# Two value matrices and the head gates share one product after the first phase, and the keys move into it

## The reference, cut to what matters

```python
u = rms_norm(h, norm1_g[layer]) * (1 + scale1) + shift1
z = u @ w_in[layer]
q_a, kc, vc, ksl, vsl, kwn, vwn, g_a, q_b, k_b, v_b, m_a, m_b = jnp.split(z, split_at, axis=-1)
k_slc = rms_norm(ksl.reshape(kv_shape), k_norm_g[layer, 1])
k_win = rms_norm(kwn.reshape(kv_shape), k_norm_g[layer, 2])
g_nsa = jax.nn.sigmoid(g_a).reshape(B, S, NSA_KV_HEADS, NSA_GROUP, 3)
y_a = nsa_attention(q_a, k_cmp, v_cmp, k_slc, vsl..., k_win, vwn..., g_nsa, rel_bias) @ w_up_nsa[layer]
y_b = stick_breaking_attention(q_b, k_b, v_b) @ w_up_sb[layer]
```

## Time and profile before

| | |
|---|---|
| runs | 1045.01 us median of 3 (1043.51 to 1045.26) |
| profiled execution | 1043.5 us, its span 1041.8 us |
| busy in the span | PE 1023.6, PEld 931.7, DVE 803.8, ACT 615.9, POOL 49.2 us |
| granted TensorE clock | 0.997 of full speed |
| traffic | 209.46 MB, mean 201 GB/s |

### The profile page before, as it was taken

One profiled execution on the slowest core, in us unless ns is written; L12 is line 12 of the kernel. 1 busy time (PEld: TensorE's weight loads), 2 busy tenths in 40 slices (PEclk: granted clock), 3 DMA queues, 4 the chain that ended last, 5 costly groups with the idle time before them and its releaser, 6 DMA issues.

```text
span 1041.8 us, 18924 instructions
## 1 busy us (share of the span) xinstructions
PE 1023.6 (98%) x6894; PEld 931.7 (89%) x6894; DVE 803.8 (77%) x1478; ACT 615.9 (59%) x1145; POOL 49.2 (5%) x74
## 2 busy tenths in 40 slices
PE   6999999999999999999999999999999999999998
PEld 5999998999988888888888889899999998888887
DVE  6997988888998655598887768667877968888753
ACT  5488788446555454565664457795654466655532
POOL 1011100020100000000000100000000020000000
PEclk9999999999999999999999999999999999999999
DMA  9997755677866666666566545545334556566663
GB/s 365 415 354 266 259 187 182 212 242 245 294 193 190 185 193 188 182 185 193 189 186 194 186 143 162 162 151 172 124 122 143 164 161 201 182 189 195 183 190 114
DMA packets 58507, 209.46 MB, mean 201 GB/s; under 512 B 7055, under 2 KB 8463, under 8 KB 57912
## 3 DMA queue, kind: packets, MB, share of 16 engines
q1 hardware_dynamic: 52616, 185.24, 55.5%
q0 software_dynamic: 5808, 23.09, 6.3%
HBM read 205.14 MB, written 3.16 MB: 200 GB/s over the span
## 4 chain that ended last, share of the span: by engine, by line
PE 89%; DVE 5%; ACT 3%; DMA 1%; issue 1%; SPq 0%; DVEq 0%; ACTq 0%
PE bank L691 88%; DVE ring_rounded L1859 2%; PE bank L1038 1%; ACT rounded_rounded L1406 1%; DVE ada_ring L1915 1%; DMA ring<-in_stream 1%; DMA ada_ring<-in_ada 1%; ACT body L1565 0%; DVE x L2224 0%; DVE body L2013 0%; DVE x L2223 0%; DVE x L2151 0%; DVE body L2063 0%; DVE body L2137 0%; DVE body L2087 0%
## 5 line engine op out<-in xcount | busy, mean ns | idle before, releaser
L691 PE MATMUL bank<-u_rounded,rounded_rounded 128*128 128x256 f32 (+1 forms) x2152 | 506.8, 329 | 1.7 <-DVE ring_rounded L1859 1.3
L1859 DVE TENSOR_TENSOR ring_rounded<-ring,rounded_rounded 128x1024 fp32r<-128x1024 f32 x326 | 395.8, 1222 | 117.0 <-ACT rounded_rounded L1406 104.8
L1406 ACT ACTIVATE rounded_rounded<-ring 128x1024 fp32r<-128x1024 f32 x326 | 342.0, 1054 | 107.9 <-PE bank L691 83.3
L691 PE MATMUL bank<-u_rounded,ring_rounded 128*128 128x256 f32 x1504 | 351.0, 281 | 0.0
L691 PEld LDWEIGHTS bank<-u_rounded,rounded_rounded 128*128 128x128 f32 x2152 | 333.0, 188 | 5.1 <-issue 1.5
L691 PE MATMUL bank<-body_rounded,rounded_rounded 128*128 128x256 f32 (+1 forms) x1296 | 322.4, 336 | 2.4 <-ACT body_rounded L1718 2.3
L691 PEld LDWEIGHTS bank<-u_rounded,ring_rounded 128*128 128x128 f32 x1504 | 283.0, 188 | 37.0
L691 PE MATMUL bank<-body_rounded,ring_rounded 128*128 128x256 f32 x952 | 217.3, 280 | 0.0
L691 PEld LDWEIGHTS bank<-body_rounded,rounded_rounded 128*128 128x128 f32 x1296 | 201.8, 189 | 4.3 <-ACT body_rounded L1718 2.5
L691 PEld LDWEIGHTS bank<-body_rounded,ring_rounded 128*128 128x128 f32 x952 | 179.0, 188 | 26.3
L1662 ACT ACTIVATE part<-bank 128x256 f32<-128x256 f32 x65 | 24.9, 383 | 78.9 <-PE bank L691 78.9
(11 more groups left out here) (269 smaller groups left out, 885.9 us busy)
## 6 DMA issues: line engine op xcount, KB each, us to landing
ring<-in_stream SPq DMA_DIRECT2D x328, 512.0 KB, 3.7
ada_ring<-in_ada POOLq DMA_DIRECT2D x32, 512.0 KB, 5.2
body<-in_ada SPq DMA_DIRECT2D x8, 512.0 KB, 9.0
ada_ring<-in_ada SPq DMA_DIRECT2D x6, 512.0 KB, 8.4
mem_parts_kept<-body_rounded POOLq DMA_DIRECT2D x2, 1024.0 KB, 6.7
body_rounded<-mem_parts_kept POOLq DMA_DIRECT2D x2, 1024.0 KB, 5.1
x<-in_x_t SPq DMA_DIRECT2D x2, 512.0 KB, 4.7
body<-in_mem_t SPq DMA_DIRECT2D x2, 512.0 KB, 7.0
```

The source lines that it names most:

```text
L691: return nc.tensor.matmul(out, lhs, rhs, start=start, stop=stop, skip_group_check=True)
L1406: a(R(slot_round(q)), slot_weights(n), ACT.Copy).then_inc(slot_rounded, 1)
L1859: v.tensor_tensor(R(w), w, R(slot_round(q)), ALU.subtract).then_inc(slot_split, 1)
```

## The change

The keys `ks` and `kw` take the place of the sparse values in the first phase, in the same slots and with as many matmuls of 256 columns. After it `project_packed` makes the sparse values and the gates in one go, 128 + 128 + 24 = 280 moving columns, three blocks `k` to a slot, so that slots 16 to 18 now hold these. The gates come out with tokens on the partitions, so `ga_turn` falls away. `mem_ss` is made halfway in that product. Banks 0, 1, 2 go by the shorter `proj_names`: bank 0 now holds `x_ss`, `vsb0`, `vsw0`, `qa1`, `cmp_hid_k`, and `qa0` takes the place of `qa1` in bank 7, behind `mem_ss`. GpSimd loads the bias diagonals behind the memory's stores.

```diff
-FIRST_BANKS = {"vsb0": 0, "vsb1": 1, "vsw0": 2, "vsw1": 2, "kc": 3, "vc": 3, ...
+FIRST_BANKS = {"vsb0": 0, "vsb1": 1, "ks": 2, "kw": 2, "kc": 3, "vc": 3, ...
+AFTER_FIRST = {"vsw0": 0, "vsw1": 1}
-    out = ["ga", "ks", "kw", "qa0", "qa2", "qa3"]
+    out = ["qa1", "qa2", "qa3"]
     out += ["cmp_hid_k", "cmp_hid_v", "ma0", "cmp_turn_k", "cmp_turn_v"]
-    out += ["ga_turn", "ma1", "cmp_out_k", "cmp_out_v", "ma2", "ma3", "ma4"]
+    out += ["ma1", "cmp_out_k", "cmp_out_v", "ma2", "ma3", "ma4"]
+            def project_packed(names, k, lhs, halfway):
+                ps = [claim(n) for n in names]
+                hi, lo = lhs
+                for i in range(k):
+                    if i == k // 2:
+                        halfway()
+                    if i % PACK == 0:
+                        chunk = at["chunk"]
+                        w_hi, w_lo = take(SLOT)
+                    c = slice(i % PACK * PACKED, (i % PACK + 1) * PACKED)
+                    for t in range(TT):
+                        at_t = slice(t * P, (t + 1) * P)
+                        ins = mm(ps[t][:, 0:PACKED], R(hi[:, i, at_t]), w_hi[:, c], i == 0)
...
+                        mm(ps[t][:, 0:PACKED], R(hi[:, i, at_t]), w_lo[:, c])
+                        ins = mm(ps[t][:, 0:PACKED], R(lo[:, i, at_t]), w_hi[:, c], stop=i == k - 1)
-            project("ga", KD, u_parts)
-            project("ks", KD, u_parts)
...
-            project("kw", KD, u_parts)
+            project_packed(("vsw0", "vsw1"), KD, u_parts, sum_memory)
             sum_squares("ks", "halves")
...
             load_ada(0, ADA_RING)
-            pool.wait_ge(bias_stored, 16)
-            pool.dma_start(bias, ...).then_inc(loaded["bias"], 16)
             load_ada(ADA_RING, ADA_RING + ADA_IN_KEYS)
...
             pool.dma_start(mem_parts_kept[1], R(mem_n_lo)).then_inc(mem_stored, 16)
+            pool.wait_ge(bias_stored, 16)
+            pool.dma_start(bias, ...).then_inc(loaded["bias"], 16)
...
             for t in range(TT):
-                output(f"vsw{t}")
...
                 spread_heads(pair_v[:, t, :, :], f"vsb{t}")
+            ahead("kc", 5)
             for w, n in enumerate(("kc", "vc")):
...
-            copy(gate_raw, "ga", bank("ga")[0:24, 0:T])
+            ahead("kc", 6)
+            square("ks")
+            square("kw", T)
             key_blocks(0)
-            square("ks")
-            row_inv("mem_ss")
-            square("kw")
+            row_inv("mem_ss", 1)
+            ahead("kc", 7)
+            for t in range(TT):
+                output(f"vsw{t}", 3)
...
             key_blocks(2)
             inv_rms("ks", HD, None)
```

More of the change, by code:

```diff
@@ L43 @@
 SLOT = 8
+GA = 24
+PACKED = 2 * P + GA
+PACK = SLOT * P // PACKED
 RAW_GATES = 4
@@ L115, in stream_chunks @@
     for k in range(KD):
-        for c in (C_VS, C_VW, *(C_VB + j * P for j in range(4)), C_KC, C_VC):
+        for c in (C_KS, C_KW, *(C_VB + j * P for j in range(4)), C_KC, C_VC):
             out.append(("w_in", span(k * P), span(c)))
@@ L120, in stream_chunks @@
                 out.append(("w_in", span(k * P), span(c + b * P)))
-    stationary("w_in", span(C_GA), full)
-    for c in (C_KS, C_KW):
-        stationary("w_in", span(c), full)
+    for j in range(-(-KD // PACK) * SLOT):
+        out.append(("values_and_gates", j, None))
     for b in range(4):
@@ L261, in plan_psum @@
     where, used = {}, [0] * 8
-    for name, b in [*BEFORE_FIRST.items(), *FIRST_BANKS.items()]:
+    for name, b in [*BEFORE_FIRST.items(), *FIRST_BANKS.items(), *AFTER_FIRST.items()]:
         where[name] = (b, used[b])
@@ L348, in long_names @@
 def long_names():
-    return ["mem_ss", "qa1"] + [f"sbo{b}" for b in range(3)]
+    return ["mem_ss", "qa0"] + [f"sbo{b}" for b in range(3)]
 def later_long_names():
@@ L456, in build @@
         table = sb("table", [33, 8])
-        gate_tanh = sb("gate_tanh", [P, TT, 24])
+        gate_tanh = sb("gate_tanh", [P, TT, GA])
         gate_t = sb("gate_t", [P, 8, 6])
@@ L514, in build @@
         gate_t_ready, tanh_ready = sem("gate_t_ready"), sem("tanh_ready")
+        gate_tanh_ready = sem("gate_tanh_ready")
         cmp_tanh_ready, cmp_rinv_ready, cmp_k_ready = sem("cmp_tanh_ready"), sem("cmp_rinv_ready"), sem("cmp_k_ready")
@@ L829, in project_tokens @@
                             done(ins, names[t])
+            def project_packed(names, k, lhs, halfway):
[11 more added lines that the diff above has]
+                        ins = mm(ps[t][:, 0:PACKED], R(hi[:, i, at_t]), w_hi[:, c], i == 0)
+                        if t == 0 and i % PACK == 0:
+                            give_back(ins, chunk)
+                        mm(ps[t][:, 0:PACKED], R(hi[:, i, at_t]), w_lo[:, c])
+                        ins = mm(ps[t][:, 0:PACKED], R(lo[:, i, at_t]), w_hi[:, c], stop=i == k - 1)
+                        if i == k - 1:
+                            done(ins, names[t])
             def sum_squares(name, matrix, n=1):
@@ L864, in _ @@
             done(mm(claim("bias")[0:8, 0:512], table[:, :], buckets[:, :], True, True), "bias")
-            first = {n: bank(n)[:, T:2 * T] if n in ("vsw1", "vc", "kb1", "kb3", "qb1", "qb3") else
+            first = {n: bank(n)[:, T:2 * T] if n in ("kw", "vc", "kb1", "kb3", "qb1", "qb3") else
                      bank(n)[:, 0:512 if n in ("vsb0", "vsb1") else T] for n in FIRST_BANKS}
             def opens(name):
-                return name in ("vsb0", "vsb1", "vsw0", "kc", "kb0", "kb2", "qb0", "qb2")
+                return name in ("vsb0", "vsb1", "ks", "kc", "kb0", "kb2", "qb0", "qb2")
             def first_tokens(names, k, w_hi, w_lo):
@@ L901, in _ @@
                 pe.wait_ge(u_ready, ROW_X * KD + k + 1)
[L902 to L908, removed]
+                give_back(mm(first["ks"], w_hi[:, 0:P], R(u[:, k, :]), k == 0), chunk)
+                mm(first["ks"], w_hi[:, 0:P], R(u_lo[:, k, :]))
+                mm(first["ks"], w_lo[:, 0:P], R(u[:, k, :]), stop=k == KD - 1)
+                both_done(first_block("kw", k, w_hi[:, P:2 * P], w_lo[:, P:2 * P]), k, "ks", "kw")
                 first_tokens(("vsb0", "vsb1"), k, w_hi[:, 256:768], w_lo[:, 256:768])
@@ L921, in _, with sum_memory @@
                     both_done(first_block(b, k, w_hi[:, at_b], w_lo[:, at_b]), k, a, b)
-            project("ga", KD, u_parts)
-            project("ks", KD, u_parts)
-            ps = claim("mem_ss")
-            pe.wait_ge(mem_summed, 3)
-            done(mm(ps[:, 0:T], mat("ones"), mem_squares[:, 0, :], True, True), "mem_ss")
-            project("kw", KD, u_parts)
+            def sum_memory():
+                ps = claim("mem_ss")
+                pe.wait_ge(mem_summed, 3)
+                done(mm(ps[:, 0:T], mat("ones"), mem_squares[:, 0, :], True, True), "mem_ss")
+            project_packed(("vsw0", "vsw1"), KD, u_parts, sum_memory)
             pe.wait_ge(loaded["mats"], 16)
@@ L959, in cmp_turn @@
                             True, True), f"cmp_turn_{n}")
[L961 to L965, removed]
             def cmp_out():
@@ L1325, in _ @@
             load_ada(0, ADA_RING)
-            pool.wait_ge(bias_stored, 16)
-            pool.dma_start(bias, bass.AP(bias_rows.tensor, bias_rows.offset, [[1, P], [512, 8], [1, T]])
-                           ).then_inc(loaded["bias"], 16)
             load_ada(ADA_RING, ADA_RING + ADA_IN_KEYS)
@@ L1333, in _ @@
             pool.dma_start(mem_parts_kept[1], R(mem_n_lo)).then_inc(mem_stored, 16)
+            pool.wait_ge(bias_stored, 16)
+            pool.dma_start(bias, bass.AP(bias_rows.tensor, bias_rows.offset, [[1, P], [512, 8], [1, T]])
+                           ).then_inc(loaded["bias"], 16)
             pool.wait_ge(bias_cmp_filled, 1)
@@ L1416, in taken, with square @@
                 evacuated(act, name)
-            def square(name):
+            def square(name, first=0):
                 n = n_squares[0]
@@ L1421, in square @@
                 output(name)
-                a(squares[:, n % SQ, :], bank(name)[:, 0:T], ACT.Square).then_inc(squares_ready, 1)
+                a(squares[:, n % SQ, :], bank(name)[:, first:first + T], ACT.Square).then_inc(squares_ready, 1)
             def inv_rms(name, width, last_reader):
@@ L1521, in key_blocks @@
                     free(a(pair_k[HI, 2 * b + 1, :], ps[HI, :], ACT.Copy), f"kb{b}")
-            copy(gate_raw, "ga", bank("ga")[0:24, 0:T])
+            ahead("kc", 6)
+            square("ks")
+            square("kw", T)
             key_blocks(0)
-            square("ks")
-            row_inv("mem_ss")
-            square("kw")
+            row_inv("mem_ss", 1)
+            ahead("kc", 7)
+            for t in range(TT):
+                output(f"vsw{t}", 3)
+                src = bank(f"vsw{t}")[:, 0:T].rearrange("p (r s d) -> p r s d", r=2, d=HD)
+                a(vcat[:, t, :, 0, 0:HD], src[:, :, 0, :], ACT.Copy)
+                a(vcat[:, t, :, 1, HD:P], src[:, :, 1, :], ACT.Copy)
```

(24 more changed lines are left out.)

3 lines of the change are left out of this document (1 added, 2 removed).

## The result

| | before | changed |
|---|---|---|
| median of 20 runs, us | 1044.36 (1042.05 to 1046.27) | 1047.27 (1044.08 to 1049.97) |
| profiled span, us | 1041.8 | 1045.5 |

The ratio is 1.0030, with a 95% interval of 1.0022 to 1.0037: the change makes the kernel slower by 2.3 to 3.9 us. The forecast said 2.0 us more and 1047.0. The spans of the two profiled executions differ by 3.7 us. Some 2.2 us of that is the late start of `cmp_hid_k`, which the forecast put at 2.0, and 1.4 us is a fall of TensorE's clock behind the wait ahead of it, which the forecast did not have.

The account below looks back on a forecast made before the run. TensorE bounds the kernel, with 89% of the chain. The late `cmp_hid_k` adds 2.0 us to the profiled 1043.5, making 1045.5; 1.5 us up to the median gives 1047.0, main case 1046.0 to 1047.8, full range 1043.6 to 1048.9.

Parts of the forecast that it names:

- Parts 1 and 2: TensorE: the packed product gains 2.34 us; dropping `ga_turn` and the wait before `ma1` counts as nothing, at most 0.9 us.
- Parts 3 to 5: ScalarE stands 2.5 us for slot 18, VectorE runs 2.4 us late from slot 20, `cmp_hid_k` starts 2.0 us later.
- One reading of the prediction: ScalarE's timeline from 58 to 106 us: one idle stretch, 1.25 us ahead of slot 19, waiting for its transfer.
- Part 5: Bank 0: `cmp_hid_k` waits for `normalise` of `qa1` until 87.3; TensorE waits some 4.4 us, starts it 2.0 us later.
- the edge of 0.2%: 0.2%, or 2.1 us, is about what a measurement can tell from no change; the forecast sits there.
- Part 6: GpSimd's queue at 55 us: the bias load hardly delayed slot 18, so its absence there counts as nothing.
- that rival: Bias load behind the second store lands late, holding up modulation loads from about 14.3 us; at 17 us 1049.2; chance 0.14.

Follow-up runs that it names:

- order_kc_norm: Changed kernel with ScalarE rounding slot 18 behind the `kc` and `vc` copies, and VectorE normalising `qa0` and `qa1` ahead of the dot products: 1041.44 us, ratio 0.9973.
- fill_clock: Changed kernel with 16 matmuls without use, of 256 columns, in TensorE's wait ahead of `cmp_hid_k`: 1045.48 us, ratio 1.0015.
- bias_old: Changed kernel with the load of the bias diagonals at its old place, behind the first three modulation loads: 1047.87 us, ratio 1.0036.
- order_kc: Changed kernel with ScalarE copying `kc` and `vc` first and rounding slot 18 behind them, as before the change: 1045.89 us, ratio 1.0016.
- kc_norm_bias: order_kc_norm with the load of the bias diagonals at its old place: 1042.16 us, ratio 0.9980 to the kernel before.
- order_kc_fill: Changed kernel with the edits of order_kc and fill_clock together: 1044.78 us, ratio 1.0004 to the kernel before.
- norm_only: Changed kernel with only VectorE's order of order_kc_norm, ScalarE as in the changed kernel: 1044.17 us, ratio 0.9996.

## Why the prediction was right, and what it lacked

**Parts 1 and 2, TensorE's gain: right, and not paid out.** From 62.75 to 69.33 stand 48 packed matmuls and the memory's sum (0.25 us, as from 68.36 in the earlier trace rows to 68.61, where the next product begins): (6.58 - 0.25) / 48 = 0.132 us each, against the 0.131 by columns. The gain of 2.3 us is there; order_kc_norm pays out 1.4 of it. Nothing came of `ga_turn`, as said: from `ma0`'s readout to the first `nsa_turn` it takes 42.6 us in the changed kernel (97.93 to 140.51) and 42.7 before (94.21 to 136.95). TensorE no longer spends there the 0.9 us of `ga_turn` and of the wait for `cmp_turned`, but it waits 0.91 us for VectorE's `body` and 0.16 us for ScalarE instead.

**Parts 3 to 5, the late slot 20 and the bank: right to 0.3 us.** Forecast and measured: slot 18 landing 62.4 and 62.65, slot 20 rounded 70.9 and 70.94, VectorE idle 2.4 and 2.57 us, memory's norm from 73.1 and 73.18, bank free 87.3 and 87.37, `cmp_hid_k` 87.3 and 87.62. The experiments take it apart: without ScalarE's stop 24.87 becomes 23.14 us, without the dot products ahead of `qa1` 23.01, without both 21.29. Each undoes about 1.8 us, and within the 0.4 us of such counts they add up. TensorE's waits ahead of `cmp_hid_k` come to 3.8 us (0.59, 0.87, 0.16 and 2.18), against some 4.4; the first 1.6 of them lay not at the splits of slots 20 to 22, as forecast, but at `qa0`'s bank and at the squares. One reading of the prediction holds only in part, and its sum does not rest on it: ScalarE has a single idle stretch up to 71 us, but not up to 106, for it stands 1.26 us ahead of 81.74, waiting for TensorE.

**The step that was missing: the clock behind the wait.** Part 5 found that TensorE would wait some 4.4 us ahead of `cmp_hid_k`, and priced this at the lateness of its end only. Of it 2.18 us lay in one piece, and behind that the granted clock was 0.53 and then 0.50, the 1.2 GHz level, at which `cmp_hid_k` ran: 1.39 us more. Fill_clock gives this back while the wait stays. The sum should have been 2.0 + 1.4 = 3.4 in an execution where the clock falls. It does not fall in all: in the profiles it fell behind such a wait in the changed kernel and in bias_old, and held in order_kc. The clocks of the timed runs give a measure: on average 0.9956 in the 20 of the changed kernel, 0.9969 and 0.9965 in the 28 and 33 of the kernel before that stand beside the experiments. The difference, 0.0009 to 0.0013, is 0.6 to 0.8 of a fall's 0.0016 in a run, by estimate 0.8 to 1.1 us. With the 2.0 that makes 2.8 to 3.1, against a measured 2.9 by the medians and 3.1 by the ratio. With this term the forecast would have stood clear of the edge of 0.2% at which it put itself.

**Part 6, the bias load: right.** bias_old shows the same landing of slot 18, so the bias waited its turn behind the modulation loads of its own queue. The rule of the Trainium skill ("DMA: Bandwidth & Descriptors", section "Queues, rings and completion order") that a ring's descriptors are taken in order agrees with the 2.69 and 2.62 us. The bias took 11.4 us to land at its new place (84.86 to about 96.3), within the 14.3 from which that rival would have decided. The prediction had allowed it at most 6.9 us with nothing ahead of it; the second store, 1 MB, had left 0.5 us before it. And the price of that rival has a slip that the sum does not use: at 17 us the chain would lose 17 - 14.3 = 2.7 us, with the slack already taken off, not 2.2.

**What stays open.** order_kc_norm gained 1.9 to 3.8 us by the timed runs, but its profile explains 1.4 up to `ma0`. Further on, its profiled execution kept its clock at a place where that of the kernel before lost it, which is worth 1.5 us (the last heading). But over its 11 timed runs the clock is 0.9970 on average, and 0.9969 in those of the kernel before beside them: the gain in the median is not made of fewer falls. Where the other 0.5 to 2.4 us of it come from is not shown.

## What to carry to other kernels

A cheaper product on the busiest engine shifts the question to whoever frees its next bank: here two lags on the way there (a rounding whose data had not landed, put ahead of other work, and two dot products ahead of a norm) each cost about 1.8 us of the 2.3 that the product saved, and only with both gone did the saving show. When work is put ahead in an engine's strict order, look first at when its data land: what then waits behind it is late by that whole time. And price a wait of TensorE twice, by the lateness of its end and by the clock of what runs right behind it.

## What the runs showed of the hardware

The same wait of 2.2 to 2.3 us lowers TensorE's clock in one execution and not in another. It fell behind the 2.18 us of the changed kernel, and held behind the 2.20 us of order_kc. There is a second such place that no edit touches: near 620 us TensorE waits 2.3 us for ScalarE's `body_rounded`. The kernel before (timeline, then a window):

```profile
619.20 0.39 PE L691 MATMUL bank<-body_rounded,rounded_rounded 128*128 128x256 f32 x1 [2.32 <-ACT body_rounded L1718]
```

```profile
620.00:622.00 2.00, 2.00 (x6) 1.55 (x6) 1.22 (x1) 0.40 (x1) 0.00 (x0) 0.50 0.03 8
```

order_kc_norm, at the same place:

```profile
619.06 0.39 PE L694 MATMUL bank<-body_rounded,rounded_rounded 128*128 128x256 f32 x1 [2.32 <-ACT body_rounded L1735]
```

```profile
620.00:622.00 2.00, 2.00 (x14) 1.84 (x14) 1.23 (x1) 0.90 (x3) 0.00 (x0) 1.00 0.00 0
```

After the same wait, 6 matmuls in two us at a clock of 0.50 and 14 at 1.00. From this product to a short stop of TensorE near 730 us it takes 111.1 us in the first (619.20 to 730.26) and 109.6 in the second (619.06 to 728.63), 1.5 us less. Of the ten profiled executions seven lost their clock there, and fill_clock, order_kc_norm and kc_norm_bias did not. That covers the rest of the 2.6 us by which the span of fill_clock fell.

A third place is the start of the kernel, where TensorE waits 3.65 to 4.00 us up to about 16 us. The clock fell there in all ten executions. In order_kc_norm, order_kc_fill, norm_only and kc_norm_bias it is at 0.50 by 15 us, with TensorE still waiting, in the other six not before 15.5. These four are also the ones whose packed product starts late, at 63.77 to 64.25 us.

So a span alone can't settle a difference of 1 to 2 us: the ratios and the clocks of many runs, and the rows counted from a common start, did.
